# Gathering the experts' token rows already turned, with the rows as the stationary operand

## The chip, the cores and the metric

The kernel runs on one core of one Trainium2 chip. The metric is the device time of one execution in microseconds (us). The kernel before took 3209.92 us in the median of three runs (3206.77 to 3210.54).

## The reference

The program computes two transformer blocks on 512 tokens of width 1024 in float32. The last stage, which is all that the change touches, is a mixture of 64 experts. A router picks two experts for every token; each expert runs a gated layer on its tokens:

```
hid = silu(xb @ w1[e]) * (xb @ w3[e])      # xb: the expert's tokens, 64 slots x 1024; w1, w3: 1024 x 512
y   = hid @ w2[e]                          # w2: 512 x 1024
```

and a token's two results are added with their gates. `xb` is a selection of rows of `hn`, the normalised tokens (512 x 1024).

## The kernel before, in words

The weights of each expert are three pieces of 2 MB (`w1`, `w3`, `w2`), 192 in all, which SyncE (SP) loads in a fixed order into eight slots of SBUF (`load_piece`, line 603). A load into a slot is issued when the piece that lay there has been used: `release` (line 682) gives the slot on, and SP waits for TensorE's last matmul on it. So TensorE sets when loads may start, and loads set when TensorE may go on. The slots go by names such as `low_pair`, `memory_norms`, `xT`, `highs`.

The rows of two experts are fetched together, as "pair" q (experts 2q and 2q+1, 64 slots each, 128 columns in all). The selection is a matrix of zeros and ones, `chosen` (`chosen_dve`, line 3202; 4 tiles of 128 tokens x 128 slots), and `hn` is held as two float32r parts, `hn_high` and `hn_low`. Three steps turn them into `xeT`, the operand that the experts' matmuls need (1024 features on the partitions in 8 groups of 128, slots along the free side):

1. `gather_pe` (line 2878): two banks of PSUM; in each, 4 token tiles x 2 parts = 8 float32r matmuls with `chosen` stationary (128x128) and 512 columns of `hn` moving. The result is the selected rows, 128 slots x 1024.
2. `rows_act` (line 3032): ScalarE copies the two banks into the buffer `rows`.
3. `rows_T_pe` (line 2894): 8 transposes of 128x128 on TensorE into two more banks; `rows_T_dve` (line 3118) copies them into `xeT` on VectorE.

Each engine runs its own list in order. `experts_pe` (line 2949) writes TensorE's by hand. Up to expert 2 it is: gather 0, rows_T 0, a small count, upper 0, upper 1, hidden_T 0, lower 0, gather 1, rows_T 1, hidden_T 1, lower 1, upper 2, hidden_T 2. From there it repeats, for even n: gather n/2, upper n-1, rows_T n/2, lower n-2, hidden_T n-1; for odd n: upper n-1, lower n-2, hidden_T n-1. "Upper" is an expert's products with `w1` and `w3` (16 float32 matmuls, which the trace records as 32), "hidden_T" the 4 turns of its hidden rows, "lower" the 8 matmuls with `w2` (16 records). The gather of pair q is thus issued before the upper step of the last expert of pair q-1, and `xeT` of pair q is needed one upper step later. PSUM banks are taken in turn from a list of eight (`Banks`, line 178). After expert 63 come the combination of the rows and the last norm.

A float32 matmul of the two halves of a bank runs as two column tiles side by side (`128*64`), a float32r matmul (tiles whose names end in `_rounded`) is one record.

Of the kernel before, what the change touches and what calls it, by code (L numbers as in the profile page):

```python
# [13 lines left out]
ACT = mybir.ActivationFunctionType  # L14
AX = mybir.AxisListType

P = 128
# [177 lines left out]
class Net:  # L195
# [2682 lines left out]
    def gather_pe(self, e, q):  # L2878

        ch = self.chosen[q % 2]  # L2880
        for half in range(2):
            bank = self.banks.take(e, "rows", q, half)
            e.wait_ge(*self.at("chosen", q))
            for i in range(NT):
                e.wait_ge(*self.at("hn_split", i))
            for i in range(NT):
                for part, hn in enumerate((self.hn_high, self.hn_low)):
                    ins = e.matmul(bank[:, :], self.rounded(ch[:, i, :, :].rearrange("p a c -> p (a c)")),
                                   self.rounded(hn[:, i, half * BANK:(half + 1) * BANK]),
                                   start=(i == 0 and part == 0), stop=(i == NT - 1 and part == 1))  # L2890
            ins.then_inc(*e.tick("pe", "rows", q, half))
            self.banks.give(("rows", q, half), "rows", q, half)

    def rows_T_pe(self, e, q):
        for half in range(2):
            bank = self.banks.take(e, "xeT", q, half)
            e.wait_ge(*self.at("rows", q, half))
            self.transposes(e, bank, [self.rows[:, half * BANK + j * P:half * BANK + (j + 1) * P] for j in range(4)]
                            ).then_inc(*e.tick("pe", "xeT", q, half))
            self.banks.give(("xeT", q, half), "xeT", q, half)  # L2900

    def hidden_pe(self, e, n, wg, wu):
# [46 lines left out]
    def experts_pe(self, e):  # L2949
        e.begin("experts")  # L2950
        last = range(self.dense - 3, self.dense)
        piece = {int(self.slots[n][0]): ("used", n) for n in last}
        high = {self.split_rank[n] % 3: ("used", n) for n in last}
        p01, p2h0, h12, memory = self.pair_slots
        self.add_slot("low", self.low_pair, ("pe", "m_gate", "retention", KD - 1))
        self.add_slot("norms", memory, ("pe", "m_gate", "retention", KD - 1))
        self.add_slot("tail", self.tail_pair, ("pe", "m_branch", "retention", KD - 1))
        self.add_slot("mT", self.mT_pair, ("merge_out", "summed", 1, NT - 1))
        self.add_slot("01", p01, piece[0], piece[1])
        self.add_slot("20", p2h0, piece[2], high[0])  # L2960
        self.add_slot("12", h12, high[1], high[2])
        self.add_slot("xT", self.xT[:, :, :].rearrange("p k s -> p (k s)"), ("pe", "router"))
        assert len(self.slots) == self.dense + FIRST_PIECES

        self.gather_pe(e, 0)
        self.rows_T_pe(e, 0)
        self.count_pe(e)
        self.upper_pe(e, 0)
        self.upper_pe(e, 1)
        self.hidden_T_pe(e, 0)  # L2970
        self.lower_pe(e, 0)
        self.gather_pe(e, 1)
        self.rows_T_pe(e, 1)
        self.hidden_T_pe(e, 1)
        self.lower_pe(e, 1)
        for n in range(3, EXPERTS - 1):
            if n % 2 == 0:
                self.gather_pe(e, n // 2)
            self.upper_pe(e, n - 1)
            if n % 2 == 0:  # L2980
                self.rows_T_pe(e, n // 2)
            if n == 5:
                self.slot_index_pe(e)
            if n > 3:
                self.lower_pe(e, n - 2)
            self.hidden_T_pe(e, n - 1)
        last = EXPERTS - 1
        self.lower_pe(e, last - 2)
        self.upper_pe(e, last - 1)
        self.last_upper_pe(e, last)  # L2990
        self.lower_pe(e, last - 1)
        self.hidden_T_pe(e, last)
        self.lower_pe(e, last)
# [32 lines left out]
    def lower_pe(self, e, ex):  # L3026
# [1 line left out]
        e.wait_ge(*self.at("landed", d))  # L3028
        self.out_pe(e, ex, self.expert_piece(d))
        self.release(e, d)  # L3030

    def rows_act(self, e, q):
        for half in range(2):
            e.wait_ge(*self.at("pe", "rows", q, half))
            e.activation(self.rows[:, half * BANK:(half + 1) * BANK], self.bank("rows", q, half)[:, :],
                         ACT.Copy).then_inc(*e.tick("rows", q, half))

    def silu_act(self, e, n):
        e.wait_ge(*self.at("pe", "hidden", n))
# [50 lines left out]

    def experts_act(self, e):
        e.begin("experts")
        self.rows_act(e, 0)
        self.silu_act(e, 0)
        self.hidden_T_act(e, 0)
        self.silu_act(e, 1)
        self.out_act(e, 0)
        self.rows_act(e, 1)
        self.hidden_T_act(e, 1)
        self.out_act(e, 1)  # L3100
        self.gates_act(e)
        for n in range(3, EXPERTS - 1):
            if n % 2 == 0:
                self.rows_act(e, n // 2)
            self.silu_act(e, n - 1)
            if n > 3:
                self.out_act(e, n - 2)
            self.hidden_T_act(e, n - 1)
        last = EXPERTS - 1
        self.out_act(e, last - 2)  # L3110
        self.silu_act(e, last - 1)
        self.hidden_T_act(e, last - 1)
        self.silu_act(e, last)
        self.hidden_T_act(e, last)
        self.out_act(e, last - 1)
        self.out_act(e, last)
# [25 lines left out]
    def experts_dve(self, e):  # L3142
        e.begin("experts")
        for n in range(EXPERTS + 1):
            if 0 < n < EXPERTS and n % 2 == 0:
                e.wait_ge(*self.at("local"))
                if n >= 4:
                    e.wait_ge(*self.at("pe", "rows", n // 2 - 2, 1))
                self.chosen_dve(e, n // 2, self.local[:, :, n:n + 2])
            if n == 0:  # L3150
                self.ranked_dve(e)
                self.picks_dve(e, 0)
                self.picks_dve(e, 1)
            if n >= 1:
                self.hidden_dve(e, n - 1)
            if n < EXPERTS and n % 2 == 0:
                self.rows_T_dve(e, n // 2)
            if n == 0:
                self.counts_dve(e)
                self.slots_dve(e, 0)  # L3160
            if n == 1:
                self.slots_dve(e, 1)
            if n == 4:
                self.slot_index_dve(e)
            if n == 5:
                self.gates_dve(e)
# [3 lines left out]
    def more_pe(self, e):  # L3170
        e.begin("more")
        views = self.more_views
        for j in range(MORE):
            n = EXPERTS + j
            if j % 2 == 0:
                self.gather_pe(e, n // 2)
                self.rows_T_pe(e, n // 2)
            e.wait_ge(*self.at("more_landed", j, 2))
            self.hidden_pe(e, n, *[lambda k, w=w: w[:, k, :] for w in views[0:2]])
            self.hidden_T_pe(e, n)  # L3180
            self.out_pe(e, n, views[2])

    def more_act(self, e):
        e.begin("more")
        for j in range(MORE):
            n = EXPERTS + j
            if j % 2 == 0:
                self.rows_act(e, n // 2)
            self.silu_act(e, n)
            self.hidden_T_act(e, n)  # L3190
            self.out_act(e, n)
# [16 lines left out]

    def more_chosen_dve(self, e, first):
        q = first // 2  # L3210
        e.wait_ge(*self.at("pe", "rows", q - 2, 1))
        for n in (first, first + 1):
            base = float(n * CAP)
            for i in range(NT):
                ch, tmp = self.chosen[q % 2][:, i, n - first, :], self.e15[:, i, 0:CAP]
                e.wait_ge(*e.own())
                e.tensor_scalar(self.rounded(ch), self.slot_order, base, self.slot_f[0][:, i:i + 1], ALU.add,
                                ALU.is_equal).then_inc(*e.tick())
                e.wait_ge(*e.own())
                e.tensor_scalar(tmp, self.slot_order, base, self.slot_f[1][:, i:i + 1], ALU.add, ALU.is_equal).then_inc(*e.tick())  # L3220
                e.wait_ge(*e.own())
                e.tensor_tensor(self.rounded(ch), self.rounded(ch).bitcast(F32), tmp, ALU.add).then_inc(
                    *(e.tick("chosen", q) if (n, i) == (first + 1, NT - 1) else e.tick()))
# [34 lines left out]

    def combine_act(self, e):
        e.begin("combine")  # L3260
        e.wait_ge(*self.at("pe", "rows", EXPERTS // 2 - 1, 1))
        e.dma_start(self.last_gain, self.a["norm_final_w_2"].partition_broadcast(P)).then_inc(
            *e.lands("last_norm_load", "last_norm", "gain"))
        for i in range(NT):
# [257 lines left out]
```

## Time and profile before

| | |
|---|---|
| median of 3 runs | 3209.92 us |
| the profiled execution | 3207.44 us |
| its span, first to last instruction | 3205.6 us |
| TensorE busy | 3077.5 us, 96% of the span |
| VectorE, ScalarE busy | 1372.7 us, 894.7 us |
| mean granted TensorE clock | 0.987 |
| HBM traffic | 193 GB/s over the span, 430 GB/s from about 2300 us on |

Times in rows are microseconds from the start of the span. PE is TensorE's matmuls, PEld its loads of stationary operands (they run beside PE), DVE VectorE, ACT ScalarE, SPq SyncE's queue. A busy PE is a modelled figure and says little about whether the engine could be faster. The stage of the experts is from about 2240 us to 3175 us; after it come 30 us of combination.

### The profile page before, as it was taken

The page shows a single profiled execution, that of the slowest core. Times are in us where ns is not written, and L with a number is a line of the kernel's source. Part 1 is how long each engine was busy: PE and PEld are TensorE (multiplying, and loading weights), DVE is VectorE, ACT ScalarE, POOL GpSimd, SP SyncE. Part 2 cuts the span into 40 slices and gives each one's busy share as a digit, 9 for nine tenths or more (in the row PEclk, how much of TensorE's full clock was granted, in tenths as well). Part 3 has the DMA queues.
Part 4 walks back from the last instruction along what each step waited for, and adds up shares of the span by engine and source line. Part 5 has one row for each costly group of instructions (what it writes and reads, how often), then busy time and mean ns, then how long its engine had stood idle before and what let it go on. Part 6 is the DMA issues. An engine that isn't in the chain of part 4 may idle for free.

```text
span 3205.6 us, 35084 instructions
## 1 busy us (share of the span) xinstructions
PE 3077.5 (96%) x14847; PEld 2156.0 (67%) x14847; DVE 1372.7 (43%) x2266; ACT 894.7 (28%) x1434; POOL 194.6 (6%) x182
## 2 busy tenths in 40 slices
PE   9999999999999999999999999999999999999896
PEld 7678688887767778888888887888444344344342
DVE  5675543335486553334767567535211111111112
ACT  3452332222344332222344442322111111111111
POOL 0000000000000000000211010000100000000000
PEclk9999999999999999999999999999999999999998
DMA  5123123333212222324222221226999999999997
GB/s 182 54 79 100 59 92 98 95 111 118 71 62 92 79 78 87 102 96 132 73 86 70 87 88 47 73 92 241 376 430 430 429 430 430 430 430 430 430 430 309
DMA packets 192388, 611.07 MB, mean 191 GB/s; under 512 B 13428, under 2 KB 130964, under 8 KB 167008
## 3 DMA queue, kind: packets, MB, share of 16 engines
q1 hardware_dynamic: 177728, 585.65, 47.0%
q10 hardware_dynamic: 9056, 18.83, 1.7%
q0 software_dynamic: 5440, 4.27, 0.4%
q8 instruction: 119, 1.95, 0.2%
q14 instruction: 45, 0.37, 0.0%
HBM read 600.30 MB, written 18.90 MB: 193 GB/s over the span
## 4 chain that ended last, share of the span: by engine, by line
PE 85%; DVE 9%; ACT 2%; issue 2%; DMA 1%; POOL 0%; SPq 0%; ACTq 0%; POOLq 0%; DVEq 0%
PE bank L124 81%; PE bank L127 4%; DVE gate_acc L142 3%; DMA memory_norms<-in_moe_w 1%; DVE probs L145 1%; DVE x_tok L142 1%; DVE qs L139 1%; ACT probs L130 0%; DVE aprobs L145 0%; POOL root L139 0%; DVE piece_rounded L139 0%; ACT xT_low_rounded L130 0%; DVE small L136 0%; DVE stat L157 0%; ACT piece_high_rounded L130 0%
## 5 line engine op out<-in xcount | busy, mean ns | idle before, releaser
L139 DVE TENSOR_TENSOR piece_rounded<-piece,piece_high_rounded 128x2048 fp32r<-128x2048 f32 (+2 forms) x159 | 343.6, 2163 | 532.3 <-ACT piece_high_rounded L130 532.3
L124 PE MATMUL bank<-xT_rounded,piece_high_rounded 128*128 128x512 f32 (+1 forms) x1392 | 531.1, 382 | 2.8 <-ACT xT_low_rounded L130 2.8
L124 PE MATMUL bank<-xT_low_rounded,piece_high_rounded 128*128 128x512 f32 (+1 forms) x1392 | 528.2, 379 | 0.0
L124 PE MATMUL bank<-xT_rounded,piece_rounded 128*128 128x512 f32 (+1 forms) x1392 | 528.1, 379 | 0.0
L139 DVE TENSOR_TENSOR gate_and_hidden<-gate_and_hidden,bank 64x512 f32<-64x512 f32 x64 | 69.2, 1081 | 757.0 <-ACT gate_and_hidden L130 757.0
L130 ACT ACTIVATE piece_high_rounded<-piece 128x2048 fp32r<-128x2048 f32 (+2 forms) x159 | 286.4, 1804 | 256.2 <-DMA piece<-in_ffn_w_down 101.2
L124 PEld LDWEIGHTS bank<-xT_rounded,piece_high_rounded 128*128 128x128 f32 x1392 | 261.8, 188 | 54.1 <-ACT xT_low_rounded L130 3.6
L124 PEld LDWEIGHTS bank<-xT_rounded,piece_rounded 128*128 128x128 f32 x1392 | 261.8, 188 | 49.6
L124 PEld LDWEIGHTS bank<-xT_low_rounded,piece_high_rounded 128*128 128x128 f32 x1392 | 261.8, 188 | 48.3
L130 ACT ACTIVATE gate_and_hidden<-bank 64x512 f32<-64x512 f32 x64 | 37.9, 592 | 471.4 <-PE bank L124 471.4
L142 DVE SCALAR_TENSOR_TENSOR gate_acc<-hT,cols,gate_acc 128x512 f32<-128x512 f32 x240 | 163.2, 743 | 0.0
L139 POOL TENSOR_TENSOR root<-root,power 128x1 f32<-128x1 f32 (+2 forms) x60 | 60.9, 1016 | 1429.8 <-DVE root L136 1429.8
L124 PE MATMUL bank<-low_pair,xeT 128*64 128x512 f32 x256 | 123.4, 639 | 16.1 <-issue 15.6
L124 PE MATMUL bank<-piece_high_rounded,hidT_rounded 128*128 128x512 f32 x352 | 137.2, 390 | 0.0
L124 PE MATMUL bank<-piece_high_rounded,hidT_low_rounded 128*128 128x512 f32 x352 | 137.0, 389 | 0.0
L124 PE MATMUL bank<-piece_rounded,hidT_rounded 128*128 128x512 f32 x352 | 136.9, 389 | 0.0
L124 PE MATMUL bank<-tail_pair,xeT 128*64 128x512 f32 x256 | 124.5, 643 | 12.3 <-issue 12.3
L124 PE MATMUL bank<-piece_high,xeT 128*64 128x512 f32 x256 | 122.3, 633 | 12.0 <-issue 12.0
L124 PE MATMUL bank<-highs,xeT 128*64 128x512 f32 x240 | 114.0, 631 | 9.1 <-issue 9.1
L124 PE MATMUL bank<-piece_high_rounded,xT_rounded 128*128 128x512 f32 (+1 forms) x320 | 120.5, 376 | 1.4 <-DVE piece_rounded L139 0.9
L124 PE MATMUL bank<-memory_norms,xeT 128*64 128x512 f32 x272 | 120.3, 595 | 0.1
L124 PE MATMUL bank<-piece_rounded,xT_rounded 128*128 128x512 f32 (+1 forms) x320 | 117.9, 368 | 0.0
(369 smaller groups left out, 5227.7 us busy)
## 6 DMA issues: line engine op xcount, KB each, us to landing
memory_norms<-in_moe_w SPq DMA_DIRECT2D x24, 2048.0 KB, 25.4
tail_pair<-in_moe_w SPq DMA_DIRECT2D x24, 2048.0 KB, 24.0
mT_pair<-in_moe_w SPq DMA_DIRECT2D x24, 2048.0 KB, 25.2
piece_high<-in_moe_w SPq DMA_DIRECT2D x24, 2048.0 KB, 24.6
xT<-in_moe_w SPq DMA_DIRECT2D x24, 2048.0 KB, 24.4
low_pair<-in_moe_w SPq DMA_DIRECT2D x23, 2048.0 KB, 25.2
pieces<-in_moe_w SPq DMA_DIRECT2D x23, 2048.0 KB, 25.3
highs<-in_moe_w SPq DMA_DIRECT2D x23, 2048.0 KB, 25.4
```

The source lines that it names most:

```text
L124: return self.engine.matmul(*a, **k) if self.engine is not None else Nothing()
L127: return self.engine.transpose(*a, **k) if self.engine is not None else Nothing()
L130: return self.engine.activation(*a, **k) if self.engine is not None else Nothing()
L139: return self.engine.tensor_tensor(*a, **k) if self.engine is not None else Nothing()
L142: return self.engine.scalar_tensor_tensor(*a, **k) if self.engine is not None else Nothing()
L145: return self.engine.tensor_tensor_reduce(*a, **k) if self.engine is not None else Nothing()
```

## The change

The gather's operands change places. `hn`, 128 features at a time, becomes the stationary operand and `chosen` the moving one, so that each product is 128 features x 128 slots, which is `xeT` itself. Each of the two banks now takes 4 feature groups x 4 token tiles x 2 parts = 32 matmuls with 128 moving columns, 64 for a pair in place of 16 with 512 columns. `rows_T_pe` and `rows_act` are gone with the buffer's use; `rows_T_dve` stays and reads the gather's banks. Waits that named the mark `rows` name `xeT`, which the gather now gives.

```diff
     def gather_pe(self, e, q):
         ch = self.chosen[q % 2]
         for half in range(2):
-            bank = self.banks.take(e, "rows", q, half)
+            bank = self.banks.take(e, "xeT", q, half)
             e.wait_ge(*self.at("chosen", q))
             for i in range(NT):
                 e.wait_ge(*self.at("hn_split", i))
-            for i in range(NT):
-                for part, hn in enumerate((self.hn_high, self.hn_low)):
-                    ins = e.matmul(bank[:, :], self.rounded(ch[:, i, :, :].rearrange("p a c -> p (a c)")),
-                                   self.rounded(hn[:, i, half * BANK:(half + 1) * BANK]),
-                                   start=(i == 0 and part == 0), stop=(i == NT - 1 and part == 1))
-            ins.then_inc(*e.tick("pe", "rows", q, half))
-            self.banks.give(("rows", q, half), "rows", q, half)
-
-    def rows_T_pe(self, e, q):
-        for half in range(2):
-            bank = self.banks.take(e, "xeT", q, half)
-            e.wait_ge(*self.at("rows", q, half))
-            self.transposes(e, bank, [self.rows[:, half * BANK + j * P:half * BANK + (j + 1) * P] for j in range(4)]
-                            ).then_inc(*e.tick("pe", "xeT", q, half))
+            for j in range(4):
+                cols = slice(half * BANK + j * P, half * BANK + (j + 1) * P)
+                for i in range(NT):
+                    for part, hn in enumerate((self.hn_high, self.hn_low)):
+                        ins = e.matmul(bank[:, j * P:(j + 1) * P], self.rounded(hn[:, i, cols]),
+                                       self.rounded(ch[:, i, :, :].rearrange("p a c -> p (a c)")),
+                                       start=(i == 0 and part == 0), stop=(i == NT - 1 and part == 1))
+            ins.then_inc(*e.tick("pe", "xeT", q, half))
             self.banks.give(("xeT", q, half), "xeT", q, half)
...
-    def rows_act(self, e, q):
-        for half in range(2):
-            e.wait_ge(*self.at("pe", "rows", q, half))
-            e.activation(self.rows[:, half * BANK:(half + 1) * BANK], self.bank("rows", q, half)[:, :],
-                         ACT.Copy).then_inc(*e.tick("rows", q, half))
```

All calls of `rows_T_pe` and `rows_act` are taken out, and nothing else in the lists of the engines moves.

## Rows read from the trace of the kernel before

**Rows 1.** Windows of the experts' stage: stretch, length and busy us by engine, PEclk, DMA.
```profile
2300.00:2400.00 100.00, 100.00 (x477) 41.47 (x478) 16.23 (x36) 15.64 (x31) 9.85 (x10) 1.00 1.01 430
...
2800.00:2900.00 100.00, 95.31 (x446) 41.75 (x444) 15.04 (x29) 15.03 (x29) 6.85 (x7) 0.98 1.01 430
```
**Rows 2.** Chain of waits, one early pair: start us, us, what.
```profile
2311.50 10.94 PE bank L124 x48
2322.44 1.02 PE bank L127 x8
...
2327.44 10.45 PE bank L124 x48
2337.89 0.39 PE bank L127 x4
2338.28 10.94 PE bank L124 x48
```
**Rows 3.** Chain of waits, about the first pause of TensorE.
```profile
2435.01 2.57 issue
2437.59 13.49 PE bank L124 x48
...
2467.40 10.45 PE bank L124 x48
```
**Rows 4.** Timeline of PE, gather of pair 8: start us, us, engine, instruction.
```profile
2451.40 0.50 PE L124 MATMUL bank<-hn_high_rounded,chosen_rounded 128*128 128x512 f32 x1
...
2455.00 0.39 PE L124 MATMUL bank<-hn_low_rounded,chosen_rounded 128*128 128x512 f32 x1
2455.32 0.64 PE L124 MATMUL bank<-pieces,xeT 128*64 128x512 f32 x1
```
**Rows 5.** Timeline of PE, two upper steps that begin after a pause, near the end.
```profile
3121.33 0.61 PE L124 MATMUL bank<-tail_pair,xeT 128*64 128x512 f32 x1 [1.05 <-issue]
...
3136.38 0.61 PE L124 MATMUL bank<-xT,xeT 128*64 128x512 f32 x1 [0.22 <-DMA memory_norms<-in_moe_w]
```
**Rows 6.** Timeline before the attention stage: float32r matmuls with 128 moving columns.
```profile
1548.32 1.87 PEld L124 LDWEIGHTS bank<-xT_rounded,minus_rounded 128*128 128x128 f32 x16
1548.34 1.99 PE L124 MATMUL bank<-xT_rounded,minus_rounded 128*128 128x128 f32 x16
```
**Rows 7.** Timeline of PE: float32r matmuls with 256 moving columns.
```profile
1552.04 0.28 PE L124 MATMUL bank<-xT_rounded,memT_rounded 128*128 128x256 f32 x1
...
1552.40 0.28 PE L124 MATMUL bank<-xT_rounded,memT_rounded 128*128 128x256 f32 x1
```
**Rows 8.** Timeline of all engines at the start of the experts' stage.
```profile
2239.59 0.50 PE L124 MATMUL bank<-hn_high_rounded,chosen_rounded 128*128 128x512 f32 x1
...
2244.86 1.28 DVE L133 COPY xeT<-bank 128x512 f32<-128x512 f32 x2
...
2246.29 0.61 PE L124 MATMUL bank<-low_pair,xeT 128*64 128x512 f32 x1 [0.52 <-DVE extra L136]
```
**Rows 9.** Timeline of PE, gather of pair 1 and its turns.
```profile
2264.78 0.50 PE L124 MATMUL bank<-hn_high_rounded,chosen_rounded 128*128 128x512 f32 x1
...
2270.05 0.46 PE L127 MATMUL bank<-ident,gate_and_hidden 64*128 64x64 f32 x4
```
**Rows 10.** SP's issues of weight loads about the DMA's last pause.
```profile
2282.00 0.43 SPq L166 DMA_DIRECT2D xT<-in_moe_w  x1
2295.34 0.33 SPq L166 DMA_DIRECT2D memory_norms<-in_moe_w  x1
```
**Rows 11.** DMA issues in 2295.2 to 2295.6: count, KB, us from issue to landing.
```profile
memory_norms<-in_moe_w SPq DMA_DIRECT2D x1, 2048.0 KB, 8.2
```
**Rows 12.** Windows, columns as in rows 1.
```profile
2285.00:2295.00 10.00, 10.00 (x47) 4.51 (x45) 0.00 (x0) 1.20 (x2) 0.00 (x0) 1.00 0.86 358
```
**Rows 13.** Windows: 62 turns in a row; an upper step after a pause.
```profile
2229.90:2239.60 9.70, 9.21 (x82) 8.81 (x80) 6.87 (x28) 0.00 (x0) 0.00 (x0) 1.00 1.01 432
...
2437.60:2443.60 6.00, 6.00 (x15) 1.89 (x17) 0.00 (x0) 0.00 (x0) 0.00 (x0) 0.50 1.03 439
```

More of the change, by code:

```diff
@@ L2965, in experts_pe @@
         self.gather_pe(e, 0)
-        self.rows_T_pe(e, 0)
         self.count_pe(e)
@@ L2972, in experts_pe @@
         self.gather_pe(e, 1)
-        self.rows_T_pe(e, 1)
         self.hidden_T_pe(e, 1)
@@ L2979, in experts_pe @@
             self.upper_pe(e, n - 1)
-            if n % 2 == 0:
-                self.rows_T_pe(e, n // 2)
             if n == 5:
@@ L3092, in experts_act @@
         e.begin("experts")
-        self.rows_act(e, 0)
         self.silu_act(e, 0)
@@ L3097, in experts_act @@
         self.out_act(e, 0)
-        self.rows_act(e, 1)
         self.hidden_T_act(e, 1)
@@ L3102, in experts_act @@
         for n in range(3, EXPERTS - 1):
-            if n % 2 == 0:
-                self.rows_act(e, n // 2)
             self.silu_act(e, n - 1)
@@ L3147, in experts_dve @@
                 if n >= 4:
-                    e.wait_ge(*self.at("pe", "rows", n // 2 - 2, 1))
+                    e.wait_ge(*self.at("pe", "xeT", n // 2 - 2, 1))
                 self.chosen_dve(e, n // 2, self.local[:, :, n:n + 2])
@@ L3176, in more_pe @@
                 self.gather_pe(e, n // 2)
-                self.rows_T_pe(e, n // 2)
             e.wait_ge(*self.at("more_landed", j, 2))
@@ L3186, in more_act @@
             n = EXPERTS + j
-            if j % 2 == 0:
-                self.rows_act(e, n // 2)
             self.silu_act(e, n)
@@ L3210, in more_chosen_dve @@
         q = first // 2
-        e.wait_ge(*self.at("pe", "rows", q - 2, 1))
+        e.wait_ge(*self.at("pe", "xeT", q - 2, 1))
         for n in (first, first + 1):
@@ L3260, in combine_act @@
         e.begin("combine")
-        e.wait_ge(*self.at("pe", "rows", EXPERTS // 2 - 1, 1))
+        e.wait_ge(*self.at("pe", "xeT", EXPERTS // 2 - 1, 1))
         e.dma_start(self.last_gain, self.a["norm_final_w_2"].partition_broadcast(P)).then_inc(
```

## The prediction

> **What bounds the kernel now.** I read the windows of the experts' stage first. They show two resources that look full at once: from 2300 us on TensorE is busy 95 to 100 us of each 100, and the DMA moves 430 GB/s without a gap [rows 1]. Only one of them can be the bound at a time, and the chain of waits tells which. Early on, a pair of experts takes TensorE 2338.28 - 2311.50 = 26.78 us, block on block, with no pause [rows 2]. At 2435.01 the first pause comes: 2.57 us in which TensorE waits for weights [rows 3], and such pauses go on to the end [rows 5]. Each of the two upper steps that begin at 2437.59 and at 3121.33 follows a pause, so each is timed by a landing. They belong to experts 14 and 60: 683.74 us for 46 experts, or 29.73 us for a pair [rows 3, 5]. That is the DMA's pace for six pieces of 2 MB. TensorE needs 26.78 and has 2.95 us to spare in every pair, but before 2435 it was behind, and it used that spare time to catch up.
>
> One more stretch matters. Between 2285 and 2295 the DMA is only 0.86 busy [rows 12]: a load was issued at 2282.00, the next only at 2295.34 [rows 10], when TensorE had ended the upper step of expert 3 and freed two slots. The load issued at 2295.34 landed after 8.2 us [rows 11]; a piece in a full queue costs 29.73 / 6 = 4.96 us, so a load into an idle queue costs some 3.2 us more. Up to this point TensorE leads and the DMA waits; from it on the stream of weights runs without a hole, and its end sets the end of the kernel. So whatever TensorE loses before 2295 moves the whole stream.
>
> **The price of the new gather.** What goes: the old gather lasts 2455.32 - 2451.40 = 3.92 us, that is 15 steps from the first to the last start at nearly 0.23 us, and 0.18 us over 16 of them for the change to the next block [rows 4]. The turns take 1.02 us in the chain [rows 2]; an upper step that runs into a turn instead of a lower step also ends 0.1 us later (10.94 against 3.92 + 6.92). Together 5.04 us; the rest of the pair is 26.78 - 5.04 = 21.74 us.
>
> What comes: 64 float32r matmuls with 128 moving columns, each with its own stationary load. The trace has exactly this shape: 16 such matmuls with 16 loads take 1.87 us on the load side, the last load 0.19 us long, so the step is (1.87 - 0.19) / 15 = 0.112 us [rows 6]. They are sixteen records for sixteen instructions, so it is one pass each. With 256 columns the step is (1552.40 - 1552.04) / 3 = 0.120 us [rows 7]: half the columns save almost nothing, so it is the load of 128 stationary columns that sets the pace. I take 0.112: 64 x 0.112 + 0.18 = 7.35 us. The upper end is the 256-column step, 7.86 us. The lower end is a line through the steps at 512 and 256 columns (0.233 and 0.120) carried on to 128, 0.064 us, if the load were hidden: 4.3 us.
>
> The Trainium skill (TensorE: Matmul & The Clock Gate, section "LDWEIGHTS (loading the stationary operand)") says that a load takes its number of columns divided by 1.2 GHz, 107 ns for 128, whatever the rows; by that the gather would cost 7.0 us and the end move by 7.6 us. The trace's 0.112 us a step stands just above it and decides. It is the rule that speaks against the change: four times the loads, and the quarter-length moving operand no longer hides them.
>
> **The sum.** Four terms.
> - Start. Gather 0 starts at 2239.59; its last bank now is done 7.2 us later, at 2246.8. VectorE, busy with other work until 2244.86, copies the first bank meanwhile and the second in 0.69 us (line of 1.28 us for two), and upper 0 starts at about 2247.8 in place of 2246.29 [rows 8]: +1.5. ScalarE's two copies and the turns are off this path, but VectorE hid most of them already.
> - Gather 1. From its start to the next block it was 2270.05 - 2264.78 = 5.27 us with turns and a wait for ScalarE [rows 9]; now 7.35: +2.1.
> - Gather 2, before upper 3: 7.35 - 3.92 = +3.4. The load of 2295.34 is issued 7.0 us later, and the stream of weights with it.
> - Middle. A pair now takes 21.74 + 7.35 = 29.09 us, against 29.73 for its weights. The DMA still bounds, with 0.64 us to spare in place of 2.95, so 28 pairs add nothing. TensorE was behind the stream at 2311.5 by what it made up until 2435.01, (123.5 / 26.78) x 2.95 = 13.6 us; now it is shifted by 5.9 there (7.0 less the turns of pair 2) and the stream by 7.0, so 12.5 us remain, and 12.5 / 0.64 = 20 of 28 pairs make them up. The next place where the DMA could run dry is the load after the six issued from 2295.34 on: it lands in turn if issued by about 2332.0, and it comes at 2322.44 + 5.9 + 3.4 = 2331.8. That is close; a miss costs tenths.
> - End. From 3121.33 on TensorE has only the 0.22 us pause at 3136.38 [rows 5], so it is TensorE's own work that ends the stage: gather 31 costs 3.43 more, its turns 1.12 less, and the pause of 0.22 fills: +2.1.
>
> Sum 7.0 + 2.1 = 9.1 us. Against the profiled execution (3207.44, its span 3205.6 and 1.8 around it) that is 3216.5; the median of the runs shown lies 2.5 above that execution, so I forecast 3219.0. Nothing else is added: the order of the list is kept, VectorE copies a pair's banks after the hidden rows of the expert before, as now, and those copies end about 3.2 us after the upper step while lower and hidden_T cover 3.97 us. The banks are retaken eight takes later instead of ten, one pair apart. ScalarE loses 1.2 us a pair, for which nobody waits except in pairs 0 and 1.
>
> How sharp the edge is: TensorE stays hidden while 21.74 + G is such that 28 pairs end with the stream. Gather 3 starts at 2311.43 + 5.9 and 28 x 29.09 later it is 3131.8, where the stream allows gather 31 at 3132.2 + 7.0 = 3139.2. The spare 7.4 us over 28 pairs and three early gathers is 0.24 us a gather, so G may reach 7.6 us, a step of 0.116 us. Beyond it every further 0.01 us of step costs 31 x 0.64 = 20 us.
>
> **Rivals.**
> - *TensorE becomes the bound.* At the 256-column step of 0.120 (new stationary data each time, as here [rows 7]; in rows 6 it is the same tile each time) G is 7.86 and a pair 29.60. Gather 3 starts at 2311.43 + 7.4, 28 pairs later it is 3147.6, 15.4 us late, and the end adds 2.6: +18, 3228. For it: distinct tiles; against it: 256 columns are 107 ns of streaming by themselves at 2.4 GHz.
> - *Not slower: the loads hide.* At 0.064 us a step G is 4.3, below the 5.04 that goes. The point from which this decides is a step of (5.04 - 0.18) / 64 = 0.076 us. Upper 0 is then tied to VectorE as now, gather 1 saves 1.0, gather 2 adds 0.4, the end saves 0.7 at most because the DMA bounds: about -1, 3209, no change. Against it stands the 0.112 of rows 6.
> - The Trainium skill (same page, section "Back-to-back issue gap") has about 81 ns a matmul for 128 columns in a stream of loads and matmuls. By that G would be 5.36 and the end +2, 3212, no measurable change. The trace's 0.112 for this type disagrees.
> - *The clock falls in the gather*, since the array streams for half of each step only. An upper step at half the clock costs 13.49 - 10.45 = 3.0 us more [rows 3, 13]; with one such loss in each pair, 32.1 us long, TensorE bounds and it is +99, 3309. Against it: 62 turns with 128 columns in a row keep the granted clock at 1.00, the upper level of 2.4 GHz [rows 13]; the 0.50 of the other row came after a pause of 2.57 us.
> - *Four passes*, as for float32: twice the step, 14.5 us, a pair 36.2: +230, 3440. Rows 6 speak against it; only its strided form differs.
>
> **How the numbers follow.** Forecast, DMA-bound with +7.5 to +11 us: 0.60. TensorE-bound at up to 0.121 us: 0.16. Loads hidden in part or whole (-1 to +5): 0.12. A piece of the 7.0 us absorbed at the start in a way I don't see (+2 to +6): 0.05. Clock 0.04, four passes 0.03. Range 3211 to 3230: it leaves out most of the hidden-load case and the two large ones, and steps over 0.121. What a measurement of this kernel can tell from no change is about 0.2%, 6.4 us. My forecast is 9.1, not far above it, so noise takes some of it: slower 0.75, same 0.21, faster 0.04.
>
> **What would show it.** In the profile after: 64 matmuls a gather at 0.112 us, a gather block of 7.3 to 7.4; no ScalarE copies from the gather's banks, no turns of `rows`; upper 0 starting at 2247.8; the issue of 2295.34 coming 7 us later; the DMA still at 430 GB/s in the middle, TensorE without a pause until some 20 pairs in, hence fewer stretches at half clock than now; the last lower step some 9 us later. Wrong: a step under 0.076 or over 0.116, upper steps at 0.85 us a pair of records in each gather's wake, a DMA rate below 430 between 2350 and 3100.

## The result, and the profile after

The changed kernel takes 3229.42 us in the median (3226.59 to 3230.76), the kernel before 3210.23 us beside it (3206.77 to 3212.58). The ratio is 1.0065, with an interval of 1.0052 to 1.0077. That is 19.2 us slower, where 9.1 were forecast. The time lies inside the range given, near its upper end; the sum behind it is short by half.

The profiled execution took 3226.59 us, its span is 3224.7. Windows of it (stretch, length and busy us by engine, PEclk, DMA share, GB/s), which answer to [rows 1, 12, 13]:

```profile
2290.80:2303.10 12.30, 12.30 (x66) 12.18 (x66) 0.00 (x0) 0.00 (x0) 0.00 (x0) 0.57 0.73 308
2303.10:2304.50 1.40, 1.40 (x5) 0.51 (x6) 0.00 (x0) 0.00 (x0) 0.00 (x0) 0.50 0.00 0
2326.60:2333.90 7.30, 7.30 (x68) 7.23 (x66) 0.00 (x0) 0.87 (x2) 0.99 (x1) 1.00 1.01 429
...
2800.00:2900.00 100.00, 97.23 (x554) 49.10 (x550) 15.43 (x27) 9.85 (x20) 5.87 (x6) 1.00 1.01 430
```

The first and the third row are both a gather of 64 matmuls. Gather 3 (third row) takes 7.3 us at full clock. Gather 2 (first row) takes 12.3, with a mean granted clock of 0.57, and the DMA runs out of work beside it: 308 GB/s, and nothing at all in the 1.4 us that follow. In the middle of the stage (last row) the DMA still moves 430 GB/s and TensorE has pauses again.

Its chain of waits (start us, us, what), which answers to [rows 2, 3]:

```profile
2288.76 1.03 issue
2289.79 0.91 DVE chosen_rounded L139 x4
2290.69 0.04 issue
2290.74 24.33 PE bank L124 x112
...
2326.66 17.74 PE bank L124 x112
2344.41 0.39 PE bank L127 x4
2344.80 10.45 PE bank L124 x48
2355.24 0.39 PE bank L127 x4
2355.64 17.74 PE bank L124 x112
...
2692.47 0.12 issue
```

A line of 112 is a gather (64), an upper step (32) and a lower step (16). It takes 17.74 us for pairs 3 and 4, and 24.33 for pair 2. A pair lasts 2355.64 - 2326.66 = 28.98 us against the DMA's 29.73, and the first pause comes at 2692.47.

The timeline of PE in gather 2 shows where those 6.6 us arise:

```profile
2289.81 0.46 PE L127 MATMUL bank<-ident,gate_and_hidden 64*128 64x64 f32 x4 [1.76 <-DVE gate_and_hidden L139]
2290.74 0.33 PE L124 MATMUL bank<-chosen_rounded,hn_high_rounded 128*128 128x128 f32 x1 [0.47 <-DVE chosen_rounded L139]
...
2291.91 0.27 PE L124 MATMUL bank<-chosen_rounded,hn_high_rounded 128*128 128x128 f32 x1
2292.02 0.28 PE L124 MATMUL bank<-chosen_rounded,hn_low_rounded 128*128 128x128 f32 x1
...
2295.05 0.41 PE L124 MATMUL bank<-chosen_rounded,hn_low_rounded 128*128 128x128 f32 x1
2295.27 0.41 PE L124 MATMUL bank<-chosen_rounded,hn_high_rounded 128*128 128x128 f32 x1
...
2302.73 0.41 PE L124 MATMUL bank<-chosen_rounded,hn_low_rounded 128*128 128x128 f32 x1
2303.08 1.12 PE L124 MATMUL bank<-memory_norms,xeT 128*64 128x512 f32 x1
```

TensorE waits 1.76 us before hidden_T 2 and 0.47 us before the gather. The gather starts with steps of 0.11 us; at about 2292.4 the granted clock falls from 2.4 to 1.2 GHz, the steps become 0.21 us, and stay so to the gather's last matmul. Only in upper 3 does the clock rise again (2306.1). SP's issues (queue, tile, count), which answer to [rows 10]:

```profile
2288.45 0.44 SPq L166 DMA_DIRECT2D xT<-in_moe_w  x1
2311.68 0.33 SPq L166 DMA_DIRECT2D memory_norms<-in_moe_w  x1
```

The load that came at 2295.34 now comes at 2311.68.

### The profile page after: what moved, and what is told of

It is laid out like the page before. It is cut to its first block, busy times and chain, and to the rows that moved or that the text cites. A ratio compares the mean times of both kernels' runs of the same rounds, so it can differ in the third digit from the quotient of the medians.

```text
span 3224.7 us, 37611 instructions
## 1 busy us (share of the span) xinstructions
PE 3136.4 (97%) x16127; PEld 2262.6 (70%) x16127; DVE 1372.6 (43%) x2266; ACT 856.6 (27%) x1370; POOL 195.1 (6%) x182
## 4 chain that ended last, share of the span: by engine, by line
PE 87%; DVE 8%; ACT 2%; issue 1%; DMA 1%; POOL 0%; ACTq 0%; SPq 0%; POOLq 0%; DVEq 0%
PE bank L124 84%; PE bank L127 3%; DVE gate_acc L142 3%; DVE probs L145 1%; DVE x_tok L142 1%; DVE qs L139 1%; ACT probs L130 0%; DVE aprobs L145 0%; POOL root L139 0%; DVE piece_rounded L139 0%; ACT xT_low_rounded L130 0%; DVE small L136 0%; DVE stat L157 0%; ACT piece_high_rounded L130 0%; DVE weigh L139 0%
## 5 line engine op out<-in xcount | busy, mean ns | idle before, releaser
L124 PE MATMUL bank<-chosen_rounded,hn_high_rounded 128*128 128x128 f32 x1024 | 236.8, 279 | 0.5 <-DVE chosen_rounded L139 0.5
L124 PE MATMUL bank<-chosen_rounded,hn_low_rounded 128*128 128x128 f32 x1024 | 235.2, 280 | 0.0
L124 PEld LDWEIGHTS bank<-chosen_rounded,hn_high_rounded 128*128 128x128 f32 x1024 | 199.8, 195 | 3.5 <-issue 0.8
L124 PEld LDWEIGHTS bank<-chosen_rounded,hn_low_rounded 128*128 128x128 f32 x1024 | 200.0, 195 | 0.0
L124 PE MATMUL bank<-piece_high_rounded,xT_low_rounded 128*128 128x512 f32 (+1 forms) x320 | 117.7, 368 | 0.0
```

The source lines that it names most:

```text
L124: return self.engine.matmul(*a, **k) if self.engine is not None else Nothing()
```

## The experiments

All times are medians with the range, beside the kernel before on the same chip. "The critical issue" is SP's issue that lay at 2295.34 [rows 10].

**1. The kernels again.** The changed kernel once more, and later the kernel before once more for a second profile.

> The changed kernel once more. Theory A: the clock falls to half in the gather of pair 2, because TensorE has just idled some 2 us before it, and does not rise again before the next upper step; this costs 6.4 us and the stream of weights moves by 7.0 + 6.4. Then the half-clock stretch is there again near 2290 us and the time is +16 to +20 over the kernel before. Rival N: the stretch at half clock was chance of one execution; then it is missing in this profile and the time is +9 to +13.

3228.97 us (3226.23 to 3231.56) against 3210.19: ratio 1.0059 (1.0045 to 1.0072). In this profile too the clock falls in gather 2, at 2294.9, for 13.7 us; the gather takes 12.03 us and the critical issue comes at 2313.80. It is no accident of one execution: seven profiles here are of kernels that have the new gather 2 in this place and nothing before it to keep TensorE busy, and all seven show it (six for 13.7 us, one for 17.1).

> The kernel before, once more, for a second profile. Theory A: no stretch at half clock in the gather of pair 2, or one of 3.4 us at most, since the old gather's 512 columns raise it again. Also to see where gather 0 starts: 2.9 to 5.0 us of the changed kernel's time lay ahead of it, in code that both share; if that is chance, this run's start may lie anywhere from 2236 to 2245.

3211.90 us. From this profile first the chain of waits, then one window (columns as above), then SP's issue:

```profile
2285.18 1.03 issue
2286.21 0.91 DVE chosen_rounded L139 x4
2287.11 0.04 issue
2287.16 12.55 PE bank L124 x48
...
3175.90 3.67 PE bank L124 x16
```
```profile
2288.00:2291.00 3.00, 3.00 (x8) 2.33 (x8) 0.00 (x0) 0.52 (x1) 0.00 (x0) 0.50 1.00 407
```
```profile
2299.75 0.33 SPq L166 DMA_DIRECT2D memory_norms<-in_moe_w  x1
```

The kernel before can lose the clock here as well (0.50 in the window): its gather 2 took 5.46 us in place of 3.92, and the clock was back after 3.4 us, at 2291.1, still within the gather; upper 3 then took its usual 7.02 us. Four profiles here have the old gather 2 in this place; two show the fall (this one and that of "pairs 3 to 31" in experiment 3), two don't. So the fall is not new. With the new gather it came in every profile, and above all it costs more. This profile is also the better partner for the changed kernel's, because gather 0 starts at 2242.46 in one and 2242.48 in the other (2239.59 in the first profile of before):

| us | before, second profile | after | difference |
|---|---|---|---|
| gather 0 starts | 2242.46 | 2242.48 | 0.0 |
| upper 0 starts | 2249.16 | 2250.72 | +1.6 |
| hidden_T 2 starts | 2286.23 | 2289.81 | +3.6 |
| upper 3 starts | 2292.62 | 2303.08 | +10.5 |
| critical issue | 2299.75 | 2311.68 | +11.9 |
| `memory_norms` lands, 168 loads later | 3140.7 | 3153.6 | +12.9 |
| last lower step starts | 3175.90 | 3190.76 | +14.9 |
| time | 3211.90 | 3226.59 | +14.7 |

**2. Keep TensorE busy ahead of gather 2.** In the wait before hidden_T 2, 16 transposes into a spare bank:

```diff
             if n > 3:
                 self.lower_pe(e, n - 2)
+            else:
+                self.keep_busy_pe(e, "busy_hidden", 16)
```

> The changed kernel with 16 turns of the identity (1.7 us of TensorE, into a bank of their own) between the upper step and hidden_T of expert 2, where TensorE idles 1.9 us waiting for VectorE. Theory A: TensorE no longer idles ahead of the gather of pair 2, the granted clock stays at 1.00 through it, the gather lasts 7.3 us and not 12.3, and the time is 5 to 7 us under the changed kernel's. Rival N: no difference from the changed kernel. Rival D, the weights' stream is slow in the changed kernel for a reason of its own (TensorE's 2500 more instructions to fetch): also no difference, and the landings' pace stays as it is.

3218.63 us (3216.80 to 3223.40): ratio to before 1.0029 (1.0018 to 1.0040), +8.4 us, and 10.3 below the changed kernel beside it. The chain of waits:

```profile
2286.90 1.08 issue
2287.98 0.91 DVE chosen_rounded L139 x4
2288.89 0.04 issue
2288.93 17.81 PE bank L124 x112
```

The line that was 24.33 us is 17.81, the gather 7.29, the granted clock 1.00 throughout. The critical issue comes at 2303.35, 8.0 after [rows 10]; gather 0 started 1.0 later here, so 7.0 are left, as forecast. With the fall gone, the kernel stands near where the forecast's sum had put it (+8.4 for +9.1).

**3. Which gathers cost what.** The new gather for pairs 0 to 2 only, for pairs 3 to 31 only, and for all but pair 2; the other pairs keep the old gather, ScalarE's copy and the turns.

```diff
+    def turned(self, q):
+        return q < 3          # or: q >= 3; q != 2
     def gather_pe(self, e, q):
+        if self.turned(q):
+            return self.turned_gather_pe(e, q)
```

> The new gather for pairs 0, 1 and 2 only; pairs 3 to 31 gather in the old way, with the copies to rows and the turns. Theory A and the forecast's terms: the start is all of the cost but 2: +7.0 for the three gathers ahead of the load that restarts the stream, +6.4 if the clock falls, so +12 to +15 in all, without the end's 2. Rival D: the cost lies along the 28 pairs of the middle, then this kernel is near +7 and the changed one's 19 need the middle.

> The new gather for pairs 3 to 31, the old one with copies and turns for pairs 0, 1 and 2. Theory A: the start as in the kernel before, the middle hidden behind the DMA (a pair takes 29.0 us of TensorE against 29.7 for its weights), the end +2: +1 to +4 in all. Rival D: +6 to +12, since every pair of the middle adds something.

> The changed kernel with pair 2 alone gathered in the old way (16 matmuls with 512 moving columns, copies to rows, turns). Theory A: gather 2 alone carries 3.4 us of length and 6.4 us of lost clock, so this kernel is some 10 us under the changed one, at +5 to +8 over the kernel before (1.5 + 2.0 for gathers 0 and 1, 2 at the end, up to 1.5 if the clock falls for a short time in the old gather). Rival: each of the three early gathers carries a third of the cost: +12 to +14.

| new gather for | median (range), us | ratio (interval) | against before | gather 2, us | clock in it |
|---|---|---|---|---|---|
| pairs 0 to 2 | 3222.57 (3221.68 to 3223.49) | 1.0038 (1.0024 to 1.0051) | +12.4 | 12.32 | falls for 13.7 us |
| pairs 3 to 31 | 3213.71 (3211.05 to 3218.32) | 1.0014 (1.0005 to 1.0023) | +3.5 | 5.47 | falls for 3.4 us |
| all but 2 | 3218.59 (3215.11 to 3221.62) | 1.0029 (1.0018 to 1.0041) | +10.1 | 3.93 | 1.00 |

Three gathers at the start cost 12.4 us and twenty-nine later ones 3.5. That is the shape of the forecast: only what stands ahead of the critical issue, and the one at the end, moves the end. But the three were to cost 7.0; the fall in gather 2 adds the rest. The whole change costs 18.8 to 19.2, and leaving it out of pair 2 alone takes away about 9 of these, near the 3.4 + 6.4 = 9.8 of that gather's steps. What is left should then have been some 1.5 + 2.0 + 1.0 + 1.9 = 6.4 us; +10.1 was measured, above what the expectation allowed. Its profile fits the steps (critical issue 2299.57, 4.2 after [rows 10], of which 0.7 lies ahead of the stage), its median doesn't: see what stays open, below.

**4. What sets the step of 0.112 us.** Ten series of 24 float32r matmuls each, with other numbers of stationary and moving columns, ahead of the stage; and 200 of the 128 by 128 shape at the end.

```diff
-        self.keep_busy_pe(e, "busy_routing", 50)
+        self.step_series_pe(e)
...
+    SERIES = ((128, 128), (128, 64), (128, 32), (64, 128), (64, 64), (32, 128), (128, 192), (128, 256), (128, 384), (128, 512))
...
+        for s, m in self.SERIES:
+            for j in range(24):
+                row = self.hn_high[:, j % 2, :]
+                at = (j % 4) * P
+                ins = e.matmul(bank[0:s, 0:m], self.rounded(row[:, at:at + s]), self.rounded(row[:, 512:512 + m]),
+                               start=True, stop=True)
...
```

> The changed kernel with two probes. First, in the router's stage the 50 turns that keep TensorE busy are replaced by ten series of 24 float32r matmuls, with the stationary columns and the moving columns of each series as 128/128, 128/64, 128/32, 64/128, 64/64, 32/128, 128/192, 128/256, 128/384, 128/512 (TensorE is needed later there, so the stage grows by some 20 us). Theory L, the load of 128 stationary columns sets the pace: 128/64 and 128/32 step at 0.11 us like 128/128, and 64/128 at half of it. Theory M, a short moving operand runs at two cycles a column: 64/128 steps at 0.11 like 128/128, 128/64 at about half, and 128/192 at 0.16. Second, in the last stage, where TensorE has idled over 10 us and its clock is at half, 200 float32r matmuls of 128 by 128 on a spare bank. Theory A: they do not raise the granted clock, each takes 0.213 us to the end (43 us in all, which lengthens the kernel). Rival: the clock rises within the first 7 us and the rest step at 0.112.

Windows of this kernel: in the series of 128 stationary and 128 moving columns, of 128 and 32, of 64 and 128, two in that of 64 and 64, one in that of 128 and 192, and two in the 200 at the end:

```profile
2233.73:2236.35 2.62, 2.62 (x26) 2.62 (x25) 2.15 (x8) 0.00 (x0) 0.00 (x0) 1.00 0.99 425
...
2239.90:2244.90 5.00, 5.00 (x26) 5.00 (x25) 0.00 (x0) 0.00 (x0) 0.00 (x0) 0.50 0.99 423
2245.10:2247.50 2.40, 2.40 (x24) 2.40 (x25) 0.00 (x0) 0.00 (x0) 0.00 (x0) 0.50 0.99 423
...
2247.70:2248.30 0.60, 0.60 (x9) 0.60 (x8) 0.00 (x0) 0.00 (x0) 0.00 (x0) 0.50 0.95 410
2248.40:2249.30 0.90, 0.90 (x18) 0.90 (x18) 0.00 (x0) 0.00 (x0) 0.00 (x0) 1.00 0.93 382
...
2250.85:2253.40 2.55, 2.55 (x26) 2.55 (x24) 0.00 (x0) 0.00 (x0) 0.00 (x0) 1.00 0.06 26
...
3236.00:3246.00 10.00, 10.00 (x47) 10.00 (x48) 9.13 (x11) 3.37 (x6) 1.27 (x3) 0.50 0.78 315
...
3266.00:3278.00 12.00, 12.00 (x58) 12.00 (x58) 0.00 (x0) 0.00 (x0) 0.00 (x0) 0.50 0.00 0
```

From first to last start of eight of the series (the clock changes within the other two, those with 64 moving columns, see below):

| stationary columns | moving columns | step, us | granted clock |
|---|---|---|---|
| 128 | 128 | 0.113 | 1.00 |
| 128 | 192 | 0.113 | 1.00 |
| 128 | 256 | 0.120 | 1.00 |
| 128 | 384 | 0.174 | 1.00 |
| 128 | 512 | 0.228 | 1.00 |
| 32 | 128 | 0.060 | 1.00 |
| 128 | 32 | 0.213 | 0.50 |
| 64 | 128 | 0.108 | 0.50 |

Between 128 and 192 moving columns nothing changes, and at half clock 64 stationary columns take half the step of 128. So a load of 128 float32r columns sets the pace of the new gather: 0.213 us at 1.2 GHz is 256 cycles, 0.107 at 2.4 GHz, and 0.005 more in the record. The Trainium skill (TensorE: Matmul & The Clock Gate, section "LDWEIGHTS (loading the stationary operand)") divides the columns by 1.2 GHz, which makes an estimate of 107 ns for 128, and the full clock's 0.112 bears it out; but it ties the load to a fixed 1.2 GHz, and here the step doubles to 0.213 when the granted clock halves.

The last two windows show the other thing: 200 matmuls of this shape that began at half clock ran 42.9 us to the end, and the clock was at 0.50 throughout. And in the second series (128 stationary, 64 moving) the clock fell, at 2238.1, while TensorE issued one matmul after another without a pause. It was back at 2248.3, in the series of 64 stationary and 64 moving columns, again without a pause and with nothing wider behind it than the 24 matmuls of 64 and 128. So a narrow moving operand alone doesn't decide; what was seen to stay down is the shape of the new gather, 128 by 128.

**5. What the clock does beside wider matmuls.** The same at the end with other widths: 100 matmuls with 512 moving columns, 150 with 256, both begun at half clock; and 200 with 128 put right behind the last lower step, at full clock.

```diff
+        for _ in range(150):      # 100 with 4 * P; 200 with P
+            ins = e.matmul(self.psum[0][:, 0:2 * P]..., x, x.unsqueeze(1).broadcast_to([P, 2, P]), start=True, stop=True)
```

> The changed kernel with one probe: in the last stage, with the clock at half after more than 10 us of idling, 100 float32r matmuls with the same 128 stationary columns but 512 moving columns. Theory A: the clock rises to full after 3 to 7 us (step from 0.43 to 0.23), because a long moving operand is what raises it; the rival, that the last stage keeps the clock down whatever runs, has 0.43 to the end.

> The changed kernel with 150 float32r matmuls of 128 stationary and 256 moving columns in the last stage, with the clock at half after more than 10 us of idling. If what counts is that columns stream (at half the clock 256 columns take 0.213 us, as long as the load of 128 stationary ones, so the array streams all the time), the clock rises after some 5 us as with 512 columns and the step falls from 0.22 to 0.12. If the many loads keep it down, it stays at 0.22 to the end.

> The changed kernel with 200 float32r matmuls of 128 stationary and 128 moving columns right behind the last lower step, where the clock is at full. Theory A in its narrow form (these matmuls do not raise a fallen clock but keep a full one, as the 29 later gathers of 7.3 us suggest): the step stays 0.112 us for all 200, 22 us in all. In its wide form (they count for too little even to keep it): the step turns to 0.213 us after some of them, beyond the 7.3 us of one gather. The kernel's time is about that of the changed one, since nothing waits for them.

Windows, first of the kernel with 512 moving columns, then with 256, then with 128 begun at full clock:

```profile
3206.95:3211.90 4.95, 4.95 (x12) 3.90 (x13) 4.24 (x5) 2.28 (x4) 0.57 (x1) 0.50 1.01 401
3212.10:3220.00 7.90, 7.90 (x36) 6.50 (x35) 7.20 (x9) 2.30 (x4) 1.37 (x3) 1.00 0.45 183
```
```profile
3210.20:3216.00 5.80, 5.80 (x27) 5.80 (x28) 4.90 (x5) 2.19 (x4) 0.57 (x1) 0.50 1.01 398
3216.40:3222.00 5.60, 5.60 (x50) 5.60 (x49) 5.39 (x6) 1.41 (x3) 1.04 (x2) 1.00 0.38 154
```
```profile
3192.00:3200.00 8.00, 8.00 (x73) 8.00 (x73) 0.00 (x0) 0.60 (x1) 0.98 (x1) 1.00 0.44 154
...
3208.00:3214.00 6.00, 6.00 (x57) 6.00 (x55) 5.69 (x7) 1.15 (x2) 1.09 (x2) 1.00 0.64 261
```

With 512 and with 256 moving columns the granted clock went from 0.50 to 1.00 in the first 5.1 and 6.1 us. With 128 it stayed where it was: begun at half (experiment 4), it stayed at half; begun at full, it kept 1.00 over the whole 22.5 us. The gathers fit this: those from pair 3 on start at full clock, with no wait ahead of them, and keep it; gather 2 starts behind two waits, the clock falls just ahead of it or in its first 2.3 us, and comes back only in upper 3.

**6. Move gather 2 behind the critical issue.** In the changed kernel, gathers 2 to 30 one upper step later (which puts gather 30 and gather 31 into the last pair) and hidden_T 2 behind upper 3; in the kernel before, the same for pair 2 alone (this is its diff).

```diff
-            if n % 2 == 0:
+            if n % 2 == 0 and n > 4:
                 self.gather_pe(e, n // 2)
             self.upper_pe(e, n - 1)
+            if n == 4:
+                self.hidden_T_pe(e, 2)
+                self.gather_pe(e, 2)
...
```

> The changed kernel in another order: each gather of pairs 2 to 30 stands after the upper step of the expert before it, not ahead, since there is no copy to rows left to hide behind that step; and hidden_T 2 stands after upper 3, where it waits for nobody. Theory A: upper 3 ends some 10 us earlier than in the changed kernel, the pause and the fall of the clock ahead of the gather go, the load that restarts the stream is issued at about 2292 us as in the kernel before; the start still costs 3.5 us for gathers 0 and 1, most of it hidden by the loads, the end 2 to 4: +2 to +6 over the kernel before. Rival N (order is of no account, the 64 matmuls cost where they are): +12 and more.

3217.32 us (3214.30 to 3219.77), ratio 1.0026 (1.0015 to 1.0037), +9.0 where at most 6 were expected. The clock stays at 1.00 and the critical issue comes at 2293.64, before [rows 10]. Yet the stream of weights is 3.7 us late near its end: the `mT_pair` that lands at 3106.5 in the kernel before lands at 3110.2 (1.6 of this lie ahead of the stage, most of the rest in one landing that took 6.7 us, at 2357.7). From there to the last lower step it is 5.5 us more than before, since gathers 30 and 31 now both stand on TensorE's path. The chain of waits:

```profile
3110.32 17.97 PE bank L124 x112
3128.29 0.39 PE bank L127 x4
3128.68 10.45 PE bank L124 x48
3139.13 0.39 PE bank L127 x4
3139.52 17.77 PE bank L124 x112
...
3158.33 13.95 PE bank L124 x64
```

Both lines of 112 hold a gather, and no line of the DMA stands between them or behind them; the last lower step begins at 3180.64.

> The kernel before with its old gather; only hidden_T 2 and gather 2 stand after upper 3, so that upper 3 frees its slots some 6 us earlier. If the stream of weights is moved by what TensorE does before that release, and by nothing else, the DMA's last pause closes and the stream ends 3 to 4 us earlier: -2 to -4 against the kernel before. If the DMA's early pause is not on the path, 0.

3204.84 us (3202.72 to 3209.55), ratio 0.9990 (0.9981 to 0.9999): 3.5 us below the kernel before, and so the fastest of the kernels here, by little. Its upper steps 2 and 3 run without the two waits between them, in one line of 80 with a lower step. Its chain of waits, then SP's issue:

```profile
2273.39 17.39 PE bank L124 x80
2290.78 0.39 PE bank L127 x4
2291.17 3.94 PE bank L124 x16
```
```profile
2290.81 0.33 SPq L166 DMA_DIRECT2D memory_norms<-in_moe_w  x1
```

The issue is 4.5 us earlier than in [rows 10], though gather 0 started 2.3 us later here (2241.91); counted from gather 0 it is 6.9 us earlier. The landing (2302.9 against 2303.5) is 0.6 us earlier, or 2.9 counted from gather 0, near the 3.5 of the medians: by then the loads ahead of it are not through yet, and the DMA has no pause left to close. This is the limit of what can be had from an earlier issue.

## Why the prediction fell short

**The step and the gather: right.** 0.112 us a step, a gather of 7.29 to 7.30 us at full clock for the forecast's 7.35. The load of the stationary operand sets it, as read from [rows 6, 7] (experiment 4).

**Start: right.** Upper 0 comes 2250.72 - 2242.48 = 8.24 us after gather 0's start, in place of 6.70: +1.5, as forecast. Its absolute start, 2250.72 for 2247.8, is later by the 2.9 us by which gather 0 is.

**Gather 1: right.** 7.29 for 5.28: +2.0 (forecast 2.1).

**Gather 2: the step that failed.** "7.35 - 3.92 = +3.4. The load of 2295.34 is issued 7.0 us later." The 3.4 are there when the clock holds (experiment 2), but it doesn't hold in this gather: 12.34 - 7.30 = 5.0 us more in the gather, and 8.39 - 7.02 = 1.4 us more in upper 3, in which the clock comes back after 3 us. So 6.4 us on top, all of it ahead of the critical issue, where each microsecond moves the end. The issue was 11.9 us later than in the matching profile of before, and the terms give that: 1.5 + 2.0 + 3.4 + 6.4 = 13.3, less the 1.5 that this profile of before lost in its own fall.

I had the mechanism as a rival, "the clock falls in the gather", and mis-framed it. I asked whether narrow matmuls in a row would lose the clock, found 62 turns that don't [rows 13], and gave it 0.04 with a price of 3.0 us in every pair. The question was what the one gather behind two waits does. The trace of before had the parts: a TensorE pause before an upper step and the clock at 0.50 after it [rows 13], and two waits just ahead of gather 2 (1.76 us at 2283.36 and 0.47 at 2284.28), though without a fall in that execution. In the old order the fall, when it came, was over in 3.4 us, within 16 matmuls with 512 moving columns, and cost 1.5; in the new one it lasts 13.7 us and is over only when the 512 columns of upper 3 run. That fits experiment 5 and the 200 matmuls of experiment 4; it was not tried on gather 2 itself.

**Middle: right, with a small remainder.** A pair takes 28.98 us (forecast 29.09), the DMA 29.73; the stage between the critical issue's landing and `memory_norms` near the end is 833.6 us against 832.7 in the first profile of before, some 1.0 more. TensorE caught up after 12.6 pairs, not 20: its spare time is 0.75 us a pair, and it was less far behind than I had worked out. A gather limit of 7.6 us was not reached. Half-clock stretches in the middle went from ten to none (fewer were forecast).

**End: right.** From that landing to the last lower step's start some 37.1 us for 35.2: +1.9 (forecast 2.1).

**The sum.** 1.5 + 2.0 + 3.4 + 6.4 + 1.0 + 1.9 = 16.2, less 1.5 for a fall in before where it happens: 14.7 against the second profile of before, which is the measured difference of those two executions (3226.59 - 3211.90). Against the first one (3207.44, without that fall, and gather 0 some 2.9 us earlier) the difference is 19.15 = 16.2 + 2.9. These 2.9 us come from common code: the clock falls at about 230 and 364 us in some executions of either kernel, and gather 0's start lay anywhere from 2236.05 to 2244.60 in the profiles (leaving out that of experiment 4, with its series ahead of it). One small sum in the prediction is off as well: with a gather of 7.0 us its four terms give 7.7 us and not 7.6; nothing rests on it.

**Left open.** The medians differ by 19.2 and 18.8 us, and the steps explain 14.7 to 16.2. The missing 3 to 4 us show in other pairs of medians too: the kernel of experiment 2 lies 10.3 below the changed one for 6.4 explained, the one with pairs 0 to 2 alone 6.4 below it for 1.0 + 1.9, and the one without pair 2 is at +10.1 for 6.4; but the kernel of experiment 2 itself stands at +8.4, where the steps give 9.8. Whether some executions lose more in the common code, or in the middle, than the profiled ones did (from the critical issue to that late landing 840.9 us in before, 841.9 in after, 844.3 in the kernel of experiment 2), one or two profiles of each can't tell. Two things are seen in single profiles. That of the 200 matmuls begun at full clock (experiment 5) has a second fall, of 3.4 us, in lower 1 behind the short wait before hidden_T 1, which makes that lower step 5.16 us long for 3.46, also ahead of the critical issue. And the 844.3 us hold five of the long landings told of in the last section where after's 841.9 hold four.

## What to carry to other kernels

Count a float32r step by the larger of two things, as the table of experiment 4 has it: the stationary columns it loads and the moving columns it streams. Where a change turns 16 wide matmuls into 64 narrow ones, it is the load that is paid, here 7.3 us for 3.9 + 1.1. Then ask of each new block not only whether it keeps the clock in a full stream, but how long it runs at half clock if the clock falls in it, behind a wait; the answer here was 5 us in one gather of 32 and 1.4 us in the block behind it, and it stood in the worst place. A few transposes in the wait take it away (-10.3 us); so does an order in which nothing that waits stands ahead of the issue that starts the stream, which gained 3.5 us even in the kernel before.

## What the runs showed of the hardware that was not expected

- Float32r matmuls with 128 stationary and 128 moving columns, issued without a pause, left a halved clock at 1.2 GHz for 42.9 us, and a full one at 2.4 GHz for 22.5 us. With 128 stationary and 64 moving columns a full clock fell in an unbroken stream, at 2238.1; with 64 and 64 it rose again in one, at 2248.3. The Trainium skill (same page, section "What's actually happening") has activity as what releases the throttle; no pause stood in the 42.9 us, so in that run a busy TensorE alone didn't release it.
- The load of 128 float32r columns follows the granted clock: 0.112 us and 0.213 us.
- In the first profiles of both kernels one weight load in 35 or 36 (after), in 47 or 48 (before), lands 6.2 to 6.8 us behind the one ahead of it, not 4.96. In both there lie 2010 to 2050 records of TensorE's (matmuls and loads) between two such loads, and the changed kernel has more records to a pair, so it meets four of them in the middle in place of three, which would be the 1.0 us of the middle term. That it is the fetching of TensorE's instructions was not tested by a run. What the profiles show for it: among the DMA queues is one of the kind "instruction" (q8), which moves one packet of 0.02 MB every 15 to 35 us, and in the first profiles of before and after every eighth of these packets lies in a long landing and the seven between them in none. Why the eighth should cost more the traces don't say.
